# Retention's group norm: mean squares laid over all partitions by one product, and the reciprocal root taken by GpSimd over 256 tokens a partition

## What is computed

```python
def retention_out(o, g, gn_w, gn_b, w_out):
    mu = o.mean(-1, keepdims=True)
    var = jnp.square(o - mu).mean(-1, keepdims=True)
    o = (o - mu) * lax.rsqrt(var + LN_EPS)
    b, h, n, dv = o.shape
    o = o.transpose(0, 2, 1, 3).reshape(b, n, h * dv) * gn_w.astype(jnp.float32) + gn_b.astype(jnp.float32)
    return (o.astype(g.dtype) * jax.nn.silu(g)) @ w_out
```

## Time and profile before

| | |
|---|---|
| median of three executions | 2363.31 us |
| the profiled execution | 2367.36 us, span 2365.2 us |
| TensorE busy | 2322.6 us (98%), granted clock 0.996 on average |
| VectorE busy | 1610.6 us (68%) |
| ScalarE busy | 976.5 us (41%) |
| GpSimd busy | 114.3 us (5%), 146 instructions |

### The profile page before, as it was taken

How to read it: one execution, slowest core, us unless ns; L and a number is a source line. 1 busy time by engine, 2 the same in 40 slices (tenths; PEclk the granted TensorE clock), 3 DMA queues, 4 the chain that set the end, 5 groups by cost and what they waited for, 6 DMA issues and landing times.

```text
span 2365.2 us, 33114 instructions
## 1 busy us (share of the span) xinstructions
PE 2322.6 (98%) x13212; PEld 2022.8 (86%) x13212; DVE 1610.6 (68%) x2189; ACT 976.5 (41%) x1497; POOL 114.3 (5%) x146
## 2 busy tenths in 40 slices
PE   7999999999999999999999999999999999999998
PEld 4988988998887888898889888889889898998996
DVE  7677658865568445686765686776588666778656
ACT  3422345652237222353224454223466335444443
POOL 1000001100100000010000020000011010000000
PEclk9999999999999999999999999999999999999999
DMA  8566655652241435444456565555556343876763
GB/s 289 174 174 199 196 194 178 180 183 72 66 149 45 150 100 151 143 137 157 164 173 198 185 205 170 166 172 188 195 169 189 121 137 105 249 241 190 225 202 123
DMA packets 469094, 396.43 MB, mean 168 GB/s; under 512 B 32430, under 2 KB 420430, under 8 KB 468686
## 3 DMA queue, kind: packets, MB, share of 16 engines
q1 hardware_dynamic: 444176, 385.93, 51.9%
q10 hardware_dynamic: 24766, 8.40, 1.4%
HBM read 390.21 MB, written 3.01 MB: 166 GB/s over the span
## 4 chain that ended last, share of the span: by engine, by line
PE 90%; DVE 7%; issue 1%; DMA 1%; ACT 1%; POOL 0%; ACTq 0%; DVEq 0%; SPq 0%
PE ps L1727 28%; PE ps L1729 28%; PE ps L1728 28%; DVE wl L1089 1%; PE ps L2028 1%; DVE st L1157 1%; PE ps L2009 1%; PE ps L1838 1%; PE ps L2109 1%; DVE nms L1530 1%; PE ps L1819 0%; DVE x_res L1243 0%; DVE tA L1229 0%; PE ps L2194 0%; DVE acc L1104 0%
## 5 line engine op out<-in xcount | busy, mean ns | idle before, releaser
L620 ACT ACTIVATE wh<-raw 128x1024 fp32r<-128x1024 f32 x560 | 591.9, 1059 | 1148.6 <-PE ps L1729 1087.8
L1089 DVE TENSOR_TENSOR wl<-raw,wh 128x1024 fp32r<-128x1024 f32 x560 | 682.7, 1223 | 553.4 <-ACT wh L620 551.7
L1727 PE MATMUL ps<-hh,wh 128*128 128x256 f32 (+1 forms) x2720 | 883.0, 325 | 1.1 <-DVE hl L1262 0.8
L1728 PE MATMUL ps<-hl,wh 128*128 128x256 f32 (+1 forms) x2720 | 880.0, 324 | 0.0
L1729 PE MATMUL ps<-hh,wl 128*128 128x256 f32 (+1 forms) x2720 | 879.9, 324 | 0.0
L1727 PEld LDWEIGHTS ps<-hh,wh 128*128 128x128 f32 x2720 | 517.5, 190 | 43.2 <-issue 1.7
L1728 PEld LDWEIGHTS ps<-hl,wh 128*128 128x128 f32 x2720 | 517.6, 190 | 40.4
L1729 PEld LDWEIGHTS ps<-hh,wl 128*128 128x128 f32 x2720 | 517.5, 190 | 40.5
L1104 DVE SCALAR_TENSOR_TENSOR acc<-araw,c,acc 128x1024 f32<-128x1024 f32 x210 | 258.7, 1280 | 54.3 <-DMA araw<-in_ada_w 52.8
L1727 PE MATMUL ps<-wh,stage_h_f 128*128 128x512 f32 x616 | 240.7, 391 | 2.0 <-DVE stage_l_f L1346 2.0
L1728 PE MATMUL ps<-wl,stage_h_f 128*128 128x512 f32 x616 | 239.8, 389 | 0.0
(11 more groups left out here) (211 smaller groups left out, 2301.0 us busy)
## 6 DMA issues: line engine op xcount, KB each, us to landing
raw<-in_ffa_w SPq DMA_DIRECT2D x204, 512.0 KB, 4.1
raw<-in_ffb_w SPq DMA_DIRECT2D x168, 512.0 KB, 3.8
raw<-in_mix_w_in SPq DMA_DIRECT2D x148, 512.0 KB, 4.5
araw<-in_ada_w SPq DMA_DIRECT2D x136, 512.0 KB, 5.3
raw<-in_ret_w_out SPq DMA_DIRECT2D x16, 512.0 KB, 4.9
raw<-in_na_fou_w_out SPq DMA_DIRECT2D x16, 512.0 KB, 4.1
raw<-in_mix_w_o SPq DMA_DIRECT2D x16, 512.0 KB, 3.5
raw<-in_ada_w SPq DMA_DIRECT2D x8, 512.0 KB, 5.6
```

What stands on the lines that cost most here:

```text
L620: A.activation(w_home(u)[0], raw[:, s, :], ACT.Copy).then_inc(w_rounded, 1)
L1089: V.tensor_tensor(low, raw[:, s, :], f(high), ALU.subtract).then_inc(w_split, 1)
L1727: T.matmul(out, a[0], b[0], start=start, stop=False)
L1728: T.matmul(out, a[0], b[1], start=False, stop=False)
```

## The change

TensorE's `variance` now takes the full tile `mean256` (128x128, all 1/256) as the stationary operand and the squares as the moving one: two matmuls of 256 columns that accumulate over the two channel halves. Each of the 128 output rows is the same sum, so tokens lie along the free axis, on every partition. VectorE adds epsilon over 128x256 into a new tile `rinv` with three buffers. GpSimd's power works on 128x256 instead of 128x2. `spread` is gone, `finish` reads `rinv` from SBUF instead of bank 7, and waits for the power itself (`r_rstd`).

```diff
-                sb("before_dft", [P, 768], scope=s)
+                rinv = sb("rinv", [P, 3, SEQ], scope=s)
...
-                    G.tensor_tensor(rve[:, t % 4], rve[:, t % 4], nhalf, ALU.pow).then_inc(r_rstd, 1)
+                    G.tensor_tensor(rinv[:, t % 3], rinv[:, t % 3], nhalf[:, 0:1].broadcast_to([P, SEQ]), ALU.pow).then_inc(r_rstd, 1)
...
                     dve.wait_ge(r_var, b + t + 1)
-                    V.tensor_scalar(rve[:, t % 4], ps[:, 6, 0:LT], EPS, None, ALU.add).then_inc(r_vare, 1)
+                    if t >= 3:
+                        dve.wait_ge(r_taken, b + t - 2)
+                    V.tensor_scalar(rinv[:, t % 3], ps[:, 6, 0:SEQ], EPS, None, ALU.add).then_inc(r_vare, 1)
...
-                    dve.wait_ge(r_spread, b + t + 1)
+                    dve.wait_ge(r_rstd, b + t + 1)
...
-                        ins = V.scalar_tensor_tensor(out=kq[:, 4 * a + h, w], in0=ps[:, 7, 0:SEQ], scalar=gnw[:, l, k:k + 1],
+                        ins = V.scalar_tensor_tensor(out=kq[:, 4 * a + h, w], in0=rinv[:, t % 3], scalar=gnw[:, l, k:k + 1],
...
-                    for q in range(LT):
-                        for a in range(2):
-                            ins = T.matmul(ps[:, 6, q:q + 1], rq2[:, t % 2, a, q * P:(q + 1) * P], mean256[:, 0:1],
-                                           start=a == 0, stop=a == 1)
+                    for a in range(2):
+                        ins = T.matmul(ps[:, 6, 0:SEQ], mean256[:], rq2[:, t % 2, a], start=a == 0, stop=a == 1)
                     ins.then_inc(r_var, 1)
-
-                def spread(t):
-
-                    pe.wait_ge(r_rstd, b + t + 1)
-                    if t >= 1:
-                        pe.wait_ge(r_taken, b + t)
-                    for q in range(LT):
-                        ins = T.matmul(ps[:, 7, q * P:(q + 1) * P], rve[:, t % 4, q:q + 1].broadcast_to([P, P]), ident[:],
-                                       start=True, stop=True)
-                    ins.then_inc(r_spread, 1)
...
-                    if t >= 2:
-                        spread(t - 2)
...
-                spread(last - 1)
                 variance(last)
...
-                spread(last)
```

## The result

The changed kernel takes 2797.57 us in the median (2796.0 to 2799.62, four runs) against 2364.03 us for the kernel before in the same comparison; the ratio is 1.1831, 95% interval 1.1816 to 1.1845. It is slower by 433.5 us. The forecast was 2692 us, 106 us too little, and the range ended at 2790, 8 us short.

A forecast was written before the change was run, and what follows sets the result against it. TensorE was taken to set the pace before, GpSimd's twelve powers in retention after. With P = 30 us, 12P - 31 gives +329 us, TensorE's 12.8 us saving included: 2363.3 + 329 = 2692 us, range 2430 to 2790.

The forecast's parts named there:

- What bounds the kernel, and who waits: Retention: TensorE sets the pace, about 5 us an item; after the change finish, VectorE and then TensorE wait for GpSimd's powers.
- the price of an element: GpSimd's power: each further element per partition costs 0.115 us, taken from the step between one and two elements.
- P: Time of one GpSimd power over 256 columns, twelve in all; forecast 30 us, between 24 and 37.
- the rival of 0.15 us or more per element: GpSimd's power costs more than forecast, up to the bound of 97 us each (3496 us); chance 0.03.
- The shared port: GpSimd's powers and VectorE's instructions with two SBUF inputs run one after the other; with them the loss is 12P - 31 us.
- a sign: In the changed kernel's profile, splits or finishes on VectorE last many us where they wait for the port.
- The second rival: Retention: powers run back to back and VectorE works beside them, ports not serialising; +292 us, 2655 us; chance 0.08.
- 12P - 68: Loss in us over both retention layers without port serialisation: (8P - 49.0) + (4P - 19.3).
- TensorE's saving: Variance and spread replaced by one product on TensorE: 1.07 us less per item, about 12.8 us for twelve items.
- Two such records: The new variance product on TensorE shows as two profile records of 0.215 us each, costed at 0.43 us.
- The first rival: GpSimd's power runs at the pace of its other work, P = 1.2 us; TensorE keeps its gain, 2350.5 us; chance 0.12.
- The point from which it decides: The kernel is faster until 12P - 31 passes zero, at P = 2.6 us.

The follow-up runs named there:

- e1_sweep: Changed kernel with the power over only 1 to 128 columns, doubling per item, in layer 0 (1, 2, 4, 8 in layer 1); one run, 2380.66 us.
- e5_port: Changed kernel plus eight VectorE additions of 128x1024, both inputs in SBUF, behind each epsilon instruction; 2798.03 us against 2797.57.
- e2_mult: Changed kernel with GpSimd's power replaced by a multiply of the same 128x256 tile; 2360.88 us against 2364.87 for the kernel before, ratio 0.9982.
- e7_lnexp2: Changed kernel with the root on ScalarE as exp(-0.5 ln(v + epsilon)), items in pairs, without GpSimd's power and VectorE's epsilon; 2359.7 us against 2364.92 before.
- e3_pow16: Changed kernel with the power over only the first 16 of 256 columns, the rest keeping the mean square; 2360.89 us.
- e6_pow32: Changed kernel with the power over only the first 32 of 256 columns, the rest keeping the mean square; 2369.21 us, ratio 1.0018.

## Why the prediction went wrong, step by step

- **What bounds the kernel, and who waits**: right. TensorE set the pace before; now finish waits for each power, TensorE waits for VectorE, and the loss lies in the two stretches of retention, 281 and 149 us.
- **The step that failed is the price of an element.** The forecast took 0.115 us, "since the step from one to two elements is the only row that shows what one more element costs", and so P = 30 us. Measured: 0.159 us and 41.1 us. The mechanism was right, the size was off, and one us of P is 12 us of time: 12 x 11.1 = 133 us. A slope over one element was carried over 254. It set the minimum of the two-element power against the median of the one-element power; the minima of both (0.688 - 0.547 = 0.141) would have given 36.5 us. The forecast's own bound for P, 37 us, was too low as well: what came is the rival of 0.15 us or more per element, which had a chance of 0.03. e1_sweep shows that small powers lie off the line by up to 0.08 us, about twice the error of 0.044 us per element that mattered.
- **The shared port**: wrong. The forecast kept VectorE's two-input instructions out for a whole power and so put 26.9 and 14.3 us of VectorE's work between powers. No split or finish lasted many us, which it named as a sign: the longest split took 2.26 us, the longest finish instruction 0.83. The second rival's way, 12P - 68, which had a chance of 0.08, is what happens: with P = 41.1 it gives 425 us, and the restarts at the lower clock, which the forecast left out, add 1.5 us in layer 0 and 2.0 in layer 1 (8.42 instead of 6.38 from the first Fourier product to the second). That leaves under 2 of the 430 us of the span. The Trainium skill's page "SBUF — State Buffer", section "SBUF: two separate sides", has the lock held for a whole instruction. A bias add of GpSimd did behave like that the earlier trace rows; a power does not, as the trace of the changed kernel and e5_port show, and the measurement decides. What was seen fits a hold while operands are read: 0.41 us of wait both for a multiply of 0.6 us and for a power of 41 us over 256 columns, and a wait that goes with the columns, 0.04 us for 32 and 0.20 for 128. That the reading of the operands is what the hold covers is an inference; where the operands are kept meanwhile was not tried.
- **The two errors had opposite signs**: +133 from the price, -37 from the port, about +5 from the clock and the rest, 329 + 133 - 37 + 5 = 430, the growth of the span. That the forecast came within 106 us is in part luck: had only the port been right, it would have been 2655.
- **TensorE's saving**: mis-sized. "Two such records" were two matmuls, and each float32 matmul is two records: 0.86 us, not 0.43, so 7.7 us and not 12.8. Of these, e2_mult kept 4.0; two waits of 0.47 us on VectorE's probs in layer 0 are part of the difference, and where the rest goes stays open. Under the powers none of it mattered.
- **The first rival** (faster, with a power at the pace of an addition) fell, and the row that was held against it pointed the right way. Its arithmetic with a cheap root was tried in e7_lnexp2: 5 us faster, not 12.8.
- **The point from which it decides**: forecast at P = 2.6 us. e3_pow16 (2.9 us) loses nothing against the multiply, e6_pow32 (5.4 us) loses 8 against it and 4 against the kernel before. It lies between, and not at the 5.7 us where 12P - 68 passes zero, since the two layers do not cancel: in layer 0 the loss begins at 49.0 / 8 = 6.1 us, in layer 1 at 19.3 / 4 = 4.8 us, and e6_pow32 lies between these two.

## What to carry to other kernels

Before one instruction replaces a small one plus a spreading product, multiply its slope per element by the new width, and compare it with the time between two uses; that product was the cheap way to spread a costly function, since it let GpSimd work on 2 columns instead of 256. A slope read from one and two elements carries an error that grows with the width, and the range has to reach well beyond the rows: here even the steeper reading of them, 0.141 us, lay below the 0.159 measured. Where a stall is hidden or not, work out each stage by itself. When a costly function must cover a full tile, look first for an engine with idle time whose cost per element is small, even if it has to switch tables.

## What was unexpected of the hardware

GpSimd's power costs 0.159 us per element and partition, 64 times an addition's 2.5 ns, from 4 to 256 columns alike, and did not change for a constant input. And GpSimd's exclusion of VectorE from the shared port ended long before the instruction did: two-input VectorE instructions of 1.22 us ran at full pace beside powers of 41 us, and the wait at a power's start was 0.04, 0.20 and 0.41 us for 32, 128 and 256 columns.
